# Input projections of a hybrid layer as seven block products per pair of column tiles (Strassen-Winograd), with block sums on GpSimd

## The chip, the cores and the metric

One Trainium2 chip, one core. The time is device microseconds of one execution of the program. The kernel before takes 1548.99 us, the median of 3 runs (1548.35 to 1551.43).

## The reference, cut to what matters

The layer takes 640 tokens (512 of one prompt, 8 x 16 of running streams), D = 1024, all float32. The change is in one product:

```
h = rmsnorm(x)                     # 640 x 1024
proj = h @ w_in                    # 1024 x 9064 columns
z, xbc, dt_raw, q, k, v, qi, ki, wi, g = split(proj)
xbc = silu(causal_conv(xbc, conv_state, conv_w, conv_b))     # 4 taps
y = rmsnorm(ssd_scan(...) * silu(z)) @ w_ssm_out             # branch a
o = dsa_attention(q, ...) @ w_attn_out                       # branch b
x = x + (sigmoid(g_a) * a + sigmoid(g_b) * b) @ w_o
x = x + hierarchical_moe(rmsnorm(x))                         # 32 experts
```

Of proj's columns, q (1024), x (2048), B and C (1024), z (2048) and the gates g (2048) make 64 column tiles of 128; each is produced as 128 output channels on the partitions by 640 tokens. k, v, ki, wi, dt and qi are projected otherwise and stay as they are.

## The kernel before, in words

The normalised, transposed input lies in SBUF as `hT` (128 x 8 x 640: 8 slices of the contraction, tokens along the free dimension). Weights pass through `wring`, a ring of three 2 MB slots (8 slices x 512 columns, four column tiles); `Ring` holds the order of the loads and the key whose products must be full before a slot is loaded anew, and SyncE (`chunks`) issues them in that order, between its other loads. `product` runs the 8 matmuls of one tile, `claim` waits until the PSUM bank of the tile before was read, `filled` signals it. `plan_banks` and `plan_group` deal out the 8 PSUM banks. A tile of q, x, B/C or z takes 8 matmuls of 512 columns (prompt) into one bank and 8 of 128 columns (streams) into a part of another; a tile of the gates takes 16 matmuls of 320 columns in two halves (`halves`).

Each engine works through one list of instructions, written by hand:

- TensorE (L1275 on): k/v, qi, transposes; query tiles 0 and 1 between the indexer's score products (`query`, L1317); indexer of the streams; query tiles 2 to 7; then four groups (`ssd_pe`, L989), each with x (4 tiles), B/C (2), z (4) and the SSM scan in 5 token tiles; gates of the first half; attention (`attention_pe`); then the dense part: branch outputs, with the gates of the second half; w_o with the router; the experts.
- ScalarE copies projections out of PSUM (`copy`, L1744; `ssd_act`, L1595): x, B and C into `raw` (two buffers of 667 columns, with the conv's old rows, L1626 and L1631), z into `zT`; after the convolution it applies Silu (L1638, L1639), and it forms the decays (`decays_act`, L1696), which come back over DRAM (`load_decays` on SyncE). `gate_act` (L1727) applies the sigmoid to gate tiles on the way out of PSUM.
- VectorE (`ssd_dve`, L1908) runs the convolution of each tile as 4 instructions (L1920, L1922) into one accumulator `acc`, and between them rounds of the top-k selection of the indexer (`top`, L2334: MAX8 and MATCH_REPLACE8, 80 rounds; `TOP_EARLY` and `TOP_UPTO` say how many run where).
- GpSimd gathers conv rows (L886), forms x * dt (L901), adds up squares (L942), issues output DMAs.

```
def product(out, chunk, m0, m, rhs, n, ks=KD, first=True, last=True):
    ...   # L1281: one matmul per slice k, all into one bank
for j in range(4):            # ssd_pe
    o = claim(pe, ("xbc", g, j))
    filled(product(o, w, j * P, P, prompt, TP), ("xbc", g, j))
```

Of the kernel before, what the change touches and what calls it, by code (L numbers as in the profile page):

```python
# [45 lines left out]
TOP_EARLY = (0, 24, 53)  # L46
TOP_UPTO = (53, 57, 65, 73, ROUNDS)
# [57 lines left out]
class Ring:  # L105
# [3 lines left out]
    def __init__(self, slots):  # L109
        self.slots, self.job, self.order, self.loads = slots, {}, [], [0] * slots  # L110

    def add(self, key, used, parts):
        s = len(self.order) % self.slots
        self.loads[s] += 16 * len(parts)
        self.job[key] = (s, self.loads[s])
        self.order.append((key, used, parts))


def plan_banks():
# [15 lines left out]
    b.add(("q", 0), any8)  # L135
    for i in range(1, 4):
        for h in range(IH):
            b.add(("pd", i, h), any8)
        if i == 2:
            b.add(("q", 1), any8)  # L140
# [15 lines left out]
    for c in range(2):  # L156
        for t in range(2 if c == 0 else 4, 4 * c + 4):
            b.add(("q", t), (2, 3, 4, 5, 6, 7))
        b.add(("qS", c), (2, 3, 4, 5, 6, 7))
# [13 lines left out]
    for s in range(-1, SB + 1):  # L173
# [6 lines left out]
        if s >= 1:  # L180
# [4 lines left out]
            b.add(("do", s - 1), (6, 7))  # L185
    for n in range(2):
        for what in ("b", "a") if n == 0 else ("ga", "gb", "a", "b"):
# [26 lines left out]

def plan_group(b, g):

    lo, hi = (0, 1, 2, 3), (4, 5, 6, 7)
    b.add(("cT", g), lo)
    b.add(("xbc", g, 0), lo)
    if g:  # L220
        b.add(("yt", g - 1), lo)
    b.add(("xbcS", g, 0), hi)
    for j in range(1, 4):
        b.add(("xbc", g, j), lo)
# [6 lines left out]
    b.add(("xbcS", g, 1), hi)  # L231
    for j in range(4, 6):
        b.add(("xbc", g, j), lo)
    for j in range(3):
        b.add(("z", g, j), lo)
    b.add(("cO", g, 0), hi)
    b.add(("cO", g, 1), hi)
    b.add(("bt", g, 0), hi)
    b.add(("bt", g, 1), hi)
    for step in range(NT + 1):  # L240
        if step < NT:
            b.add(("xt", g, step), lo)
            b.add(("cb", g, step), hi)
        if step == 0:
            b.add(("z", g, 3), lo)
        elif step == NT - 1:
            b.add(("zS", g), hi)
        if step > 0:
# [3 lines left out]
            if tt < SMP:  # L252
                b.add(("st", g, tt), hi)
            b.add(("yo", g, tt), lo if tt < SMP else (0,))
    for half in range(2):
        for j in range(2 * half, 2 * half + 2):
            for i in range(2):
                b.add(("s0", g, j, i), (1, 2, 3))
            if j == 0:
                b.add(("so", g), hi)  # L260
# [6 lines left out]
    if g == GROUPS - 1:  # L267
        b.add(("yt", g), lo)
        for c in range(4):
            for h in range(2):  # L270
                b.add(("ga", 0, c, h), lo)
        for c in range(4):
            for h in range(2):
                b.add(("gb", 0, c, h), lo)
# [4 lines left out]
def hybrid_layer(nc, x_prompt, x_sample, cache_k, cache_v, cache_kidx, state_conv, state_ssm,  # L279
# [9 lines left out]
    ring = Ring(3)  # L289
# [2337 lines left out]
```

## Time and profile before

| what | value |
|---|---|
| median of 3 runs | 1548.99 us |
| the profiled execution's own time | 1552.75 us |
| its span in the profile | 1551.0 us |
| granted TensorE clock, mean | 0.961 |
| TensorE busy | 1416.6 us, 91% |
| VectorE / ScalarE / GpSimd busy | 649.9 / 459.6 / 222.2 us |

The profile counts a float32 matmul of the program as two records, so 8 matmuls of a tile are "x16". Stages in us from the start of the span: 0 to 124 norm, k/v, indexer; 124 to 180 query tiles 2 to 7; 180 to 653 the four groups; 653 to 722 first gates; 722 to 882 attention; 882 to 1158 dense part; 1158 to 1257 w_o and router; 1257 to 1512 experts; then the output.

### The profile page before, as it was taken

Reading aid. Unit: us, or ns where it says so; the run is one execution under the profiler, and the core shown is the slowest. Engines: PE = TensorE matmul, PEld = TensorE weight load, DVE = VectorE, ACT = ScalarE, POOL = GpSimd, SP = SyncE. Lnnn points to the kernel's source line nnn. Section 1 sums busy time; section 2 is a strip of 40 time slices with the busy share of each in tenths; the row PEclk is TensorE's granted clock in tenths of the full one; section 3 lists DMA queues with packets and bytes.
Section 4 is the critical chain, followed back from the end, with each engine's and each line's share of the span. In section 5 each row is a group of like instructions: output and inputs, shape, how many; then the busy total and the mean of one; then the engine's idle time right before and its main releaser. Section 6 shows DMA issues by size and latency. Waiting matters only on the chain.

```text
span 1551.0 us, 19156 instructions
## 1 busy us (share of the span) xinstructions
PE 1416.6 (91%) x7458; PEld 895.4 (58%) x7458; DVE 649.9 (42%) x1435; ACT 459.6 (30%) x1059; POOL 222.2 (14%) x334
## 2 busy tenths in 40 slices
PE   7999999999999999999888899999999979878780
PEld 5545654764764764776566677777764545545440
DVE  3059962676776775802655511000013443211105
ACT  2161024652653653523655500010002211111112
POOL 3000000220220320312540000000000023222210
PEclk9999999999999999998999999999999979999885
DMA  8821313524433432707108420312036199999965
GB/s 235 221 80 32 109 55 99 163 94 127 148 108 102 152 111 68 198 15 232 23 17 185 152 99 0 109 55 55 0 119 264 45 363 414 415 416 415 414 262 210
DMA packets 135180, 247.43 MB, mean 160 GB/s; under 512 B 38836, under 2 KB 81572, under 8 KB 126164
## 3 DMA queue, kind: packets, MB, share of 16 engines
q1 hardware_dynamic: 124020, 215.10, 40.7%
q0 software_dynamic: 11072, 31.12, 5.6%
q8 instruction: 60, 0.98, 0.3%
q14 instruction: 28, 0.23, 0.0%
HBM read 216.50 MB, written 36.88 MB: 163 GB/s over the span
## 4 chain that ended last, share of the span: by engine, by line
PE 82%; DVE 5%; ACT 5%; issue 4%; DMA 3%; POOL 1%; SPq 0%; DVEq 0%; ACTq 0%; POOLq 0%
PE psum L1281 50%; PE psum L1559 9%; PE psum L1285 5%; PE psum L1459 4%; PE psum L1575 4%; PE psum L1313 2%; ACT arena L1744 2%; ACT arena L1823 1%; DVE arena L2053 1%; PE psum L1230 1%; PE psum L1185 1%; PE psum L1266 1%; PE psum L1090 1%; DVE arena L2468 1%; PE psum L1084 1%
## 5 line engine op out<-in xcount | busy, mean ns | idle before, releaser
L1281 PE MATMUL psum<-hT,wring 128*128 128x512 f32 (+2 forms) x2176 | 596.0, 436 | 0.7 <-issue 0.7
L1281 PEld LDWEIGHTS psum<-hT,wring 128*128 128x128 f32 x2176 | 349.7, 192 | 237.6 <-issue 196.9
L1285 PE MATMUL psum<-ident,arena 128*128 128x128 f32 (+3 forms) x950 | 141.2, 285 | 37.9 <-ACT arena L1744 12.5
L1285 PEld LDWEIGHTS psum<-ident,arena 128*128 128x128 f32 (+3 forms) x950 | 105.8, 143 | 96.2 <-issue 64.7
L1744 ACT ACTIVATE arena<-psum 128x512 f32<-128x512 f32 (+8 forms) x199 | 96.9, 535 | 198.4 <-PE psum L1281 138.0
L1281 PE MATMUL psum<-arena,wring 128*128 128x320 f32 x512 | 138.1, 431 | 0.0
L1281 PEld LDWEIGHTS psum<-arena,wring 128*128 128x128 f32 x512 | 96.6, 189 | 41.2
L1559 PE MATMUL psum<-wring,arena 128*64 128x256 f32 x608 | 79.2, 419 | 25.5 <-issue 21.7
L1559 PEld LDWEIGHTS psum<-wring,arena 128*64 128x64 f32 x608 | 52.2, 151 | 47.9 <-issue 27.8
L2475 DVE TENSOR_TENSOR arena<-psum,arena 128x128 f32<-128x128 f32 x32 | 9.3, 291 | 162.9 <-ACT arena L1893 157.4
L2398 DVE TENSOR_TENSOR arena<-psum,arena 128x320 f32<-128x320 f32 x16 | 7.9, 491 | 156.1 <-PE psum L1281 156.1
L1459 PE MATMUL psum<-wring,arena 128*128 128x512 f32 x160 | 70.6, 595 | 0.0
L1281 PE MATMUL psum<-oT,wring 128*128 128x320 f32 x256 | 69.3, 433 | 0.4 <-issue 0.4
L1922 DVE SCALAR_TENSOR_TENSOR arena<-arena,pc 128x664 f32<-128x664 f32 x72 | 67.5, 937 | 2.6
L2341 DVE MAX8 ssq<-arena 128x8 f32<-128x1040 f32 (+3 forms) x80 | 66.5, 832 | 1.9
L962 POOL DMA_DIRECT2D x_rows<-arena x5 | 2.7, 546 | 438.6 <-ACT arena L1886 438.6
L2342 DVE MATCH_REPLACE8 arena<-ssq,arena 128x1040 f32<-128x1040 f32 (+3 forms) x80 | 65.2, 815 | 0.0
L1893 ACT ACTIVATE arena<-psum 128x128 f32<-128x128 f32 x32 | 8.9, 277 | 179.5 <-PE psum L1559 166.4
L1575 PE MATMUL psum<-arena 128*64 128x512 f32 x256 | 61.0, 592 | 0.4 <-ACT arena L1895 0.4
L1281 PEld LDWEIGHTS psum<-oT,wring 128*128 128x128 f32 x256 | 48.6, 190 | 20.7 <-issue 0.6
L983 POOL DMA_INDIRECT y_rows<-arena,slot_row x32 | 32.4, 1011 | 186.6 <-ACT arena L1901 149.9
L2053 DVE CUSTOM_DVE_ANT_0 arena<-psum,arena 128x256 f32<-128x256 f32 (+3 forms) x64 | 43.3, 726 | 24.0 <-PE psum L1230 18.7
(321 smaller groups left out, 1543.7 us busy)
## 6 DMA issues: line engine op xcount, KB each, us to landing
wring<-in_w SPq DMA_DIRECT2D x38, 1024.0 KB
arena<-in_w SPq DMA_DIRECT2D x32, 1024.0 KB
wring<-in_w_in SPq DMA_DIRECT2D x13, 2048.0 KB, 7.7
hT<-in_w SPq DMA_DIRECT2D x14, 1024.0 KB
oT<-in_w SPq DMA_DIRECT2D x12, 1024.0 KB
arena<-a_rows SPq DMA_DIRECT2D x20, 512.0 KB, 4.3
arena<-in_state_ssm SPq DMA_DIRECT2D x16, 512.0 KB, 7.1
out<-arena POOLq DMA_DIRECT2D x16, 512.0 KB, 4.2
```

Of the source, the lines that this page charges most:

```text
L983: pool.indirect_dma_start(y_rows[:, :], bass.IndirectOffsetOnAxis(ap=slot_row[:, e:e + 1], axis=0), ysl[:, e % RS, :], None, bounds_check= ...
L1281: ins = mm(out, chunk[:, k, m0:m0 + m], rhs(k), start=first and k == 0, stop=last and k == ks - 1)
L1285: return nc.tensor.transpose(out, in_, ident[0:rows, 0:rows])
L1313: ins = mm(o[:, 0:SW], hT[:, k, tt * P:(tt + 1) * P], w[:, k, 0:SW], start=k == 0, stop=k == KD - 1)
L1459: ins = mm(o, mrg[:, k, t * P:(t + 1) * P], ws[n][:, k, :], start=k == 0, stop=k == KD - 1)
L1559: ins = mm(pbank(2 + e % 2)[h * SLOTS:(h + 1) * SLOTS, 0:FF].rearrange("p (c f) -> p c f", c=2), hgT[:, e % 2, k, :], w13[e % XS][:, :, k, ...
L1575: ins = mm(pbank(4 + e % 2)[m * SLOTS:(m + 1) * SLOTS, :], heT[:, e % 2, k, :], w2s[e % XS][:, k, HD2 * m:HD2 * (m + 1)], start=k == 0, st ...
L1744: release(fn(out, in_, ACT.Copy), key)
L1922: ins = stt(out=a, in0=r[:, w:w + 664], scalar=cw_col[:, w, ct:ct + 1], in1=a, op0=ALU.mult, op1=ALU.add)
L2053: release(nc.vector.tensor_tensor_reduce(out=out, in0=scores, in1=bias, scale=-ATT_SCALE, scalar=3.0e38, op0=ALU.add, op1=ALU.min, accum_o ...
L2341: link(nc.vector.max(top8, scores))
L2342: link(nc.vector.match_replace(scores, top8, scores, TAKEN))
```

## The change

Two neighbouring column tiles (256 columns) form a pair; there are 32 pairs: 4 of q, 5 in each of the four groups (x, x, B/C, z, z), 8 of the gates. A pair is split in blocks: the contraction in two halves of 4 slices, the tokens in two halves of 320, the columns in two tiles. Instead of 8 block products (32 matmuls of 320 columns) it takes seven, in the order 1, 5, 6, 3, 7, 2, 4, of 4 matmuls each. Products 1, 6, 7 and 4 go on adding into one bank, 5 and 3 into another, 2 has a third. After 1, 5 and 6 ScalarE copies the bank's present content to SBUF; VectorE forms three of the four output blocks as PSUM plus such a copy, and ScalarE copies the fourth:

```
SEVEN = (1, 5, 6, 3, 7, 2, 4)

def sum_weights(pool, key):
    ...
    tt_(s1, w[:, 0:4, P:2 * P], w[:, 4:8, P:2 * P], ALU.add).then_inc(S["sums_ready"], 1)
    tt_(s2, s1, w[:, 0:4, 0:P], ALU.subtract).then_inc(S["sums_ready"], 1)
    tt_(s4, w[:, 4:8, 0:P], s2, ALU.subtract).then_inc(S["sums_ready"], 1)
    tt_(w[:, 0:4, P:2 * P], w[:, 0:4, 0:P], w[:, 0:4, P:2 * P], ALU.subtract).then_inc(S["sums_ready"], 1)

def dense(pe, key, steps=SEVEN):
    w, (s1, s2, s4) = slot(key), weight_sums(key)
    terms = {1: (w[:, 0:4, 0:P], top_l), 5: (s1, row_sums[0]), 6: (s2, row_sums[1]), 3: (s4, low_r),
             7: (w[:, 0:4, P:2 * P], top_r), 2: (w[:, 4:8, 0:P], low_l), 4: (w[:, 4:8, P:2 * P], row_sums[2])}
    for n in steps:
        o = claim(pe, key + (n,))
        ...
        for k in range(4):
            ins = nc.tensor.matmul(o[:, 0:TH], wt[:, k, :], rows[:, k, :], start=n in (1, 5, 2) and k == 0,
                                   stop=k == 3, skip_group_check=True)
        filled(ins, key + (n,))

def pair_added(dve, key, n):          # n = 3, 7, 2
    held, i, h = {3: (6, 0, 1), 7: (5, 1, 1), 2: (1, 0, 0)}[n]
    for dst, a, b in homes(key, i, h):
        ins = nc.vector.tensor_tensor(dst, like(dst, bank(key + (n,))[:, a:b]), like(dst, stage(key, held)[:, a:b]), ALU.add)
    release(ins, key + (n,))

def pair_staged(act, key, n):         # n = 1, 5, 6: bank -> SBUF, 320 columns
def pair_crossed(act, key, fn_=ACT.Copy):     # n = 4
```

`claim` of a product that goes on in a bank waits until the product before it in that bank was read. `sum_rows` makes, once, three sums and one difference of blocks of `hT` (each 128 x 1280) on GpSimd, after the last use of qi; the block `top_r` of `hT` is overwritten.

The ring has four slots; the pairs use slots 0 and 1 in turn, each with 1 MB of weights, its sums and the staged copies beside them; a pair's weights are loaded when the pair before the last is done. Row sums lie in slot 2, slot 3 is `hT` after its last use.

Order: the pair q0 takes the places of query tiles 0 and 1 (4 products, then 3); in a group the first x pair is split by the turned stream rows and conv rows, the second z pair by scan steps 1 to 3. The gates of the second half move ahead of both branch outputs, which now run b, a, b, a (before: b, a, gates, a, b). `sum_weights` stands on GpSimd some 10 to 20 us of TensorE work ahead of its pair. Squares and gains of group g - 1 move behind the first x pair of group g, the decays of token tile 1 behind x pair 2. The top-k rounds are dealt out anew:

```
-TOP_EARLY = (0, 24, 53)
-TOP_UPTO = (53, 57, 65, 73, ROUNDS)
+TOP_Q = (22, 23, 24, 25, 26, 33, 39)
+TOP_GROUP = (46, 56, 59, 62, 65)
+TOP_GATES = (69, 74, 79, ROUNDS)
```

The experts' weight buffers are renumbered (first `wring` slot 1, then `oT`, slots 2 and 0, `hT`; before `hT` first).

TensorE, start of group 1's x tiles, before (L1281 is a projection, L1285 a transpose):

```order
L1281 MATMUL psum<-hT,wring 128x512 [waits free0,slot_loaded1]
L1281 MATMUL psum<-hT,wring 128x512 x7
L1285 MATMUL psum<-ident,arena 128x128 [waits free1,free0]
L1285 MATMUL psum<-ident,arena 128x128 x3
L1281 MATMUL psum<-hT,wring 128x128 [waits free5]
L1281 MATMUL psum<-hT,wring 128x128 x31
L1281 MATMUL psum<-hT,wring 128x512 [waits free2]
L1281 MATMUL psum<-hT,wring 128x512 x7
```

The same place now, products 5, 6, 3, then 7, 2, 4 of the first x pair (L639 is `dense`):

```order
L639 MATMUL psum<-wring 128x320 [waits sums_ready,free1]
L639 MATMUL psum<-wring 128x320 [waits sums_ready,free3]
L639 MATMUL psum<-hT,wring 128x320 [waits sums_ready,free1]
L1417 MATMUL psum<-ident,arena 128x128 [waits free0]
...
L639 MATMUL psum<-hT,wring 128x320 [waits sums_ready,free3]
L639 MATMUL psum<-hT,wring 128x320 [waits free2]
L639 MATMUL psum<-wring 128x320 [waits free3]
```

Each row now stands for a product of four matmuls; banks 3 and 1 come back after one other product, where before a bank came back after some tiles.

VectorE, group 1's x tiles, before (L1920/L1922 conv, L2341/L2342 a top-k round):

```order
L1993 TENSOR_TENSOR oT<-oT,psum 128x4x128 [waits free0,full1]
L1997 SCALAR_TENSOR_TENSOR oT<-arena,dcol,oT 128x640 [waits free1]
L1997 SCALAR_TENSOR_TENSOR oT<-arena,dcol,oT 128x640 [waits dve_chain] x3
L2000 TENSOR_TENSOR oT<-oT,arena 128x2560 [waits z_ready,dve_chain]
L1920 TENSOR_SCALAR arena<-arena,pc 128x664 [waits xs_ready,raw_ready]
L1922 SCALAR_TENSOR_TENSOR arena<-arena,pc 128x664 [waits dve_chain] x3
L2341 MAX ssq<-arena 128x8
L2342 MATCH_REPLACE arena<-ssq,arena 128x1040 [waits dve_chain]
L1920 TENSOR_SCALAR arena<-arena,pc 128x664 [waits xs_ready,raw_ready,dve_chain]
```

The same place now (L607 is `pair_added`; the convs are L2095/L2097, the rounds L2565/L2566), from the y rows of group 0 to the adds of the second x pair:

```order
L2201 SCALAR_TENSOR_TENSOR oT<-arena,dcol,oT 128x640 [waits dve_chain] x3
L607 TENSOR_TENSOR arena<-psum,wring 128x192 [waits gathered,full1,conv_done,free3,full0,dve_chain]
L607 TENSOR_TENSOR arena<-psum,wring 128x8x16
L607 TENSOR_TENSOR arena<-psum,wring 128x192 [waits full3,gathered,free1,conv_done,full0]
L2211 TENSOR_TENSOR oT<-oT,arena 128x2560 [waits z_ready]
L607 TENSOR_TENSOR arena<-psum,wring 128x320 [waits free3,full2]
L2095 TENSOR_SCALAR arena<-arena,pc 128x664 [waits free2,xs_ready,free1,raw_ready]
...
L2095 TENSOR_SCALAR arena<-arena,pc 128x664 [waits xs_ready,free3,raw_ready]
L2097 SCALAR_TENSOR_TENSOR arena<-arena,pc 128x664 [waits dve_chain] x3
L607 TENSOR_TENSOR arena<-psum,wring 128x192 [waits full1,free0,gathered,conv_done]
```

VectorE's reads of PSUM now stand between its convs and rounds, and two convs follow one another where a round stood between them.

## Rows read from the trace of the kernel before

**Rows 1.** The page: busy us, share of the span, instructions; and slices of 38.8 us, tenths.

```profile
PE 1416.6 (91%) x7458; PEld 895.4 (58%) x7458; DVE 649.9 (42%) x1435; ACT 459.6 (30%) x1059; POOL 222.2 (14%) x334
...
PEclk9999999999999999998999999999999979999885
```

**Rows 2.** The chain that ended last, in order: start us, us, what.

```profile
40.38 34.61 PE psum L1281 x128
...
243.45 5.55 DMA a_rows<-arena
...
317.34 65.66 PE psum L1281 x224
...
882.43 275.86 PE psum L1281 x1024
```

**Rows 3.** Stretches: us, busy (instructions) of PE, PEld, DVE, ACT, POOL; PEclk, DMA share, GB/s.

```profile
75.00:125.00 50.00, 47.22 (x231) 22.34 (x230) 29.85 (x80) 29.68 (x73) 0.00 (x0) 0.97 0.22 64
125.00:181.00 56.00, 56.00 (x231) 33.04 (x230) 52.50 (x129) 5.14 (x16) 0.32 (x3) 1.00 0.08 21
317.00:431.00 114.00, 112.71 (x617) 68.64 (x615) 78.67 (x122) 55.83 (x126) 21.94 (x36) 1.00 0.38 121
882.00:1158.00 276.00, 275.57 (x1026) 193.93 (x1025) 34.59 (x47) 10.58 (x20) 0.00 (x0) 1.00 0.22 73
265.00:275.00 10.00, 8.94 (x22) 4.61 (x23) 2.28 (x4) 9.89 (x26) 1.04 (x1) 0.66 1.05 260
```

**Rows 4.** Timeline of TensorE: start us, us, line, op, count [idle before, releaser].

```profile
265.35 1.20 PE L1285 MATMUL psum<-ident,arena 128*128 128x128 f32 x9 [2.00 <-ACT arena L1639]
...
267.26 0.80 PE L1061 MATMUL psum<-arena 128*128 128x128 f32 x2 [0.70 <-ACT arena L1744]
267.85 9.77 PE L1281 MATMUL psum<-hT,wring 128*128 128x512 f32 x16
```

**Rows 5.** Groups by form, ScalarE: busy us, mean ns, idle before.

```profile
L1744 ACT ACTIVATE arena<-psum 128x512 f32<-128x512 f32 x146 | 81.5, 597 | 196.8 <-PE psum L1281 138.0 <-PE psum L1285 57.2 <-PE psum L1342 1.6
L1733 ACT ACTIVATE arena<-psum 128x320 f32<-128x320 f32 x32 | 13.8, 437 | 108.4 <-PE psum L1281 101.5 <-DVE oT L2000 4.2 <-POOL arena L942 2.6
```

**Rows 6.** Groups by form, VectorE and GpSimd.

```profile
L2398 DVE TENSOR_TENSOR arena<-psum,arena 128x320 f32<-128x320 f32 x16 | 7.9, 491 | 156.1 <-PE psum L1281 156.1
L901 POOL TENSOR_TENSOR arena<-arena 128x512 f32<-128x512 f32 x20 | 20.8, 1041 | 146.7 <-DVE arena L1950 146.7
L942 POOL TENSOR_TENSOR arena<-arena 128x640 f32<-128x640 f32 x15 | 20.3, 1350 | 70.9 <-ACT arena L1687 70.0
```

**Rows 7.** Timeline of VectorE, group 1.

```profile
318.10 3.65 DVE L1997 SCALAR_TENSOR_TENSOR oT<-arena,dcol,oT 128x640 f32<-128x640 f32 x4
...
334.52 1.24 DVE L2341 MAX8 ssq<-arena 128x8 f32<-128x1040 f32 x1
...
337.13 0.57 DVE L1920 TENSOR_SCALAR arena<-arena,pc 128x664 f32<-128x664 f32 x1
337.73 2.80 DVE L1922 SCALAR_TENSOR_TENSOR arena<-arena,pc 128x664 f32<-128x664 f32 x3
...
385.60 2.11 DVE L1964 TENSOR_TENSOR arena<-arena 128x512 f32<-128x512 f32 x2
...
405.11 1.29 DVE L1964 TENSOR_TENSOR arena<-arena 128x512 f32<-128x512 f32 x2
```

**Rows 8.** Timeline of GpSimd, group 1.

```profile
385.52 1.04 POOL L901 TENSOR_TENSOR arena<-arena 128x512 f32<-128x512 f32 x1 [21.73 <-DVE arena L1950]
```

**Rows 9.** Timeline of ScalarE, group 1.

```profile
332.38 1.28 ACT L1638 ACT_TABLE_LOAD   x1
334.64 0.72 ACT L1638 ACTIVATE arena<-arena,pc 128x512 f32<-128x512 f32 x1 [0.98 <-DVE arena L1922]
...
388.07 2.44 ACT L1720 ACTIVATE arena<-arena 128x128 f32<-128x128 f32 x8
```

**Rows 10.** The page, DMA issues: line, engine, count, KB each, us to landing.

```profile
wring<-in_w_in SPq DMA_DIRECT2D x1, 1024.0 KB, 7.0
```

More of the change, by code:

```diff
@@ L155, in plan_banks @@
             b.add(("di", 1), (1,))
[L156 to L159, printed above, removed]
+    for i in range(1, 4):
+        plan_pair(b, ("q", i), (2 if i % 2 else 5, 3, 4))
     for g in range(GROUPS):
@@ L212, in plan_banks, with plan_pair @@
     return b
+def plan_pair(b, key, banks, steps=SEVEN):
+    acc, other, third = banks
+    for n in steps:
+        b.add(key + (n,), (acc if n in (1, 6, 7, 4) else other if n in (5, 3) else third,))
 def plan_group(b, g):
     lo, hi = (0, 1, 2, 3), (4, 5, 6, 7)
-    b.add(("cT", g), lo)
-    b.add(("xbc", g, 0), lo)
+    plan_pair(b, ("x", g, 0), (3, 1, 2), (1, 5, 6, 3))
     if g:
[L221 to L224, printed above, removed]
+        b.add(("yt", g - 1), (0,))
+    b.add(("cT", g), (7,))
+    plan_pair(b, ("x", g, 0), (3, 1, 2), (7, 2, 4))
+    plan_pair(b, ("x", g, 1), (0, 1, 2))
     if g == 0:
@@ L230, in plan_group @@
             b.add(("ar", i), hi)
[L231 to L239, printed above, removed]
+    plan_pair(b, ("bc", g), (3, 1, 2))
+    plan_pair(b, ("z", g, 0), (0, 1, 2))
+    b.add(("cO", g, 0), (7,))
+    b.add(("cO", g, 1), (4,))
+    b.add(("bt", g, 0), (5,))
+    b.add(("bt", g, 1), (6,))
     for step in range(NT + 1):
@@ L267, in plan_group @@
     if g == GROUPS - 1:
[L268 to L274, printed above, removed]
+        b.add(("yt", g), (0,))
+        for i, what in enumerate(("ga", "ga", "gb", "gb")):
+            plan_pair(b, (what, 0, i % 2), (0 if i % 2 else 3, 1, 2))
         for i in range(2):
@@ L727, in _ @@
                     load_decays(0, 1)
+                chunks(("z", g, 1))
+                after = [("x", g + 1, i) if g + 1 < GROUPS else ("ga", 0, i) for i in range(2)]
                 for tt in range(2, NT):
@@ L1315, in _ @@
             pe.wait_ge(consts, 3)
-            def query(t):
-                w = wait_chunk(pe, ("wq", t // 4))
-                o = claim(pe, ("q", t))
-                filled(product(o, w, (t % 4) * P, P, prompt, TP), ("q", t))
             w = wait_chunk(pe, ("wqi",))
@@ L1911, in ssd_dve, with conv @@
             y = yb[:, g % 2, :, :]
-            for j in range(6):
+            def conv(key, j):
                 u = 6 * g + j
@@ L2383, in _ @@
             newton(rt, rr, mrg[:, 0, :])
+            for what in ("ga", "gb"):
+                for i in range(2):
+                    for n_ in (3, 7, 2):
+                        pair_added(dve, (what, 1, i), n_)
             def merge(m, j):
```

610 lines of the change are left out of this document (393 added, 217 removed).

## The prediction

> **What bounds the kernel now.** I began with the page. TensorE is busy 91% of the span, the others 42, 30 and 14%, and its clock is granted at nine tenths or more in the slices of the four groups and the dense part [rows 1]. The chain of waits says the same by place: over a whole run of projections in a group it stays on TensorE for 65.66 us, and in the dense part for 275.86 us [rows 2]. The table of stretches shows that inside those stages TensorE idles hardly at all (112.71 of 114 us busy in group 1, 275.57 of 276 in the dense part) at a granted clock of 1.00, its upper level of 2.4 GHz [rows 3]. So a matmul less there is time less, and what can spoil it is an engine that hands a bank back late. VectorE is the one to watch: 52.50 of 56 us busy beside the query tiles, 78.67 of 114 in a group [rows 3].
>
> **What is removed.** The 34.61 us piece holds qi: 32 matmuls of 512 and 32 of 128 columns (two records each), so a couple costs 34.61 / 32 = 1.082 us [rows 2]. The dense part is 512 matmuls of 320 columns in 275.86 us, 0.539 each [rows 2]. A pair of q, x, B/C or z took 16 couples, 17.31 us; it takes 28 x 0.539 = 15.09, 2.22 less. A pair of the gates took 32 x 0.539 = 17.24, 2.15 less. 24 x 2.22 + 8 x 2.15 = **70.5 us** off TensorE.
>
> **What is added, and what hides it.** ScalarE makes four copies of 320 columns a pair, 4 x 0.437 = 1.75 us, where two tiles took 2 x 0.597 and two short ones: no more than before; the gates get sigmoids out of SBUF on top, hidden by 15 us of matmuls a pair [rows 5]. VectorE gets three adds a pair, at 0.491 for 320 columns; one that is split in two parts lies between that and twice that, and I take 0.65 [rows 6]: 1.8 us a pair, 58 us in all. GpSimd gets four sums of 512 columns a pair, 4 x 1.041 = 4.2 us, 133 us in all, and 4 x 2 x 1.35 = 10.8 us of row sums [rows 6]; it was busy 222 of 1551 us. The weights of a pair (1 MB) took 7.0 us to land in the one load of that size [rows 10]. 7.0 + 4.2 = 11.2 us is less than the 15.1 us of the pair between, and SyncE's `chunks` now waits for the pair before the last, so the sums should be in time; if that cover went, each pair would wait some us. The loads are the same bytes. The experts' buffers are renumbered, but as before two of five come free with w_o: nothing. The moves of squares, gains and gates cost nothing where TensorE has matmuls queued.
>
> **What the short banks cost.** Products are 4 x 0.539 = 2.16 us. A bank is wanted back one product after it was filled. ScalarE needs 0.44 for that; VectorE stands in longer work. Product 4 wants its bank 6 x 2.16 = 12.9 us after the pair's start, so VectorE must be at adds 3 and 7 (1.3 us) by 11.6. It comes from the last add of the pair before at about -1.7. Between stand two convs of 0.57 + 2.80 = 3.4 us, one Silu of 0.72 (with the streams' part about 1.1) before the second may use `acc` [rows 7, 9], and ScalarE first stages product 5, which ends at 4.3. The second conv so starts at 4.3 + 0.4 + 1.1 = 5.9, or 7.1 with a table load of 1.28 [rows 9], and ends at 9.3 to 10.5. In groups 1 to 3:
> - second x pair, no top-k round before it: in time.
> - B/C and first z pair, one round of 2.6 (334.52 to 337.13 [rows 7]): 11.9 to 13.1, late by 0.3 to 1.5; I take 0.9 each. ScalarE also has decays before B/C's conv (2.44 and more [rows 9]); bounds 0 and 3.
> - first x pair: the turned stream rows come at 9.7 us; behind them stand one operation of y of 512 columns and four of 640, 3.65 us [rows 7], then the adds 3 and 7: read at 14.9 instead of 14.0, late by 0.9.
> - second z pair, inside the scan: its staging holds up ScalarE's decays; nothing to 3 us, I take 1.5.
> - GpSimd beside VectorE: with a GpSimd sum running (385.52, 1.04 us [rows 8]) two SBUF-to-SBUF operations of VectorE took 2.11 us, without one 1.29 [rows 7]: 0.8 lost per sum. The conv is such an operation. If all four sums of three pairs lie beside convs it is 9.8 us a group; part of it falls where VectorE waits for Silu anyway. I take 2.4, bounds 0 and 9.8.
>
> That is 0.9 + 1.8 + 1.5 + 2.4 = 6.6 a group, **+19.8** for three. The Trainium skill (SBUF — State Buffer, "Who interferes with whom") makes it an exclusive lock: a VectorE instruction with two SBUF inputs waits out a GpSimd instruction that reads SBUF. By that rule the 0.8 would be up to 1.04, and the sum 2 us higher; the rows lie a little under it.
>
> Group 0: the second x pair has two rounds of the prompt before it (late 1.3, taken as half a round of the streams), B/C's three are covered by the small products of dt between; z's two rounds make it late by 3.5 (10.5 + 5.2 - 11.6 = 4.1 at most, 2.9 at least): 4.8. Its second z pair 1.5, contention 0.8. Given back is a wait of before: SyncE was held by a load's bank wait and wrote the decays only at 243.45 [rows 2]; TensorE then stood 2.00 and 0.70 us for ScalarE, and the next 8 matmuls took 9.77 us where 8 x 512 / 320 x 0.539 = 6.9 is full speed [rows 4], the clock granted there being 0.66 [rows 3]. In the new order that `chunks` waits only for an x pair. 2.0 + 0.7 + 2.9 = 5.6 back; net **+1.5**.
>
> Start: q0 stands in the indexer, where TensorE was busy 47.22 of 50 us and VectorE feeds the chain [rows 3]. Its row sums come one after the other, 2.7 us each, from the last use of qi; VectorE gets 1.8 us more: **+3** (0 to 6). Query pairs 1 to 3: rounds are cut into pieces so that the adds come in time, 7 fewer run before the groups: 0 (to 3). Gates: before the first ones 4 or 5 rounds, 13 us, just inside; after attention VectorE has the norm's reciprocal before the first adds; ScalarE a table load: **+3** in all (1 to 6).
>
> **Sum:** -70.5 + 19.8 + 1.5 + 3 + 3 = -43.2. Against the profiled execution's 1552.75 that is 1509.6; the median of the runs lies 3.8 below it, so **1506 us**. A change of 0.2% (3.1 us) is about what a measurement of this kernel can tell from none.
>
> **Rivals.**
> - *TensorE stays the bound, waits nearly vanish.* For it: the deadlines above are missed by about 1 us only. Against: they are missed on paper. -70.5 + 4 leaves 1482.
> - *VectorE becomes the bound in the groups.* All GpSimd sums beside convs and the upper bounds of the lateness: 3 x (0.9 + 3.0 + 3 + 9.8) = 50 and 5 more in group 0: 1505.8 - 19.8 + 50 + 5 = 1541. Against: VectorE's total in a group, 78.67 less five rounds (13) plus 9 of adds, stays well under 103. The Trainium skill (GPSIMD Engine Reference, "Engine selection") advises against this placing, saying two-input elementwise work belongs on VectorE, GpSimd being about 2x slower; by rows 1.041 against 0.65 (1.29 / 2) for 512 columns. On VectorE the sums would cost it 83 us more; that it isn't there speaks for the forecast.
> - *Short products don't run at 0.539.* If each of 224 products ends with a gap of 0.1 to 0.15 us because of its semaphores: 22 to 34 more, 1534. Against: the dense part changed bank every 8 matmuls at no visible cost.
> - *Slower: the clock.* Where waits grow to 2 us TensorE falls to its lower level, as at 265 to 275 [rows 3, 4]: 2.7 us of wait and 2.9 of clock. It decides if VectorE is late by 2 us or more at nearly every pair; at 20 pairs of the groups 20 x 5.6 = 112: 1552.75 - 3.8 - 70.5 + 112 = 1590. Against: group 1, with its 1.3 us of waits, keeps 1.00 [rows 3].
> - *The change does less than it says* (a pair falling back to eight products) is excluded: the listed rows show 28 matmuls a pair.
>
> **How the numbers follow.** Forecast 0.60, waits vanish 0.17, VectorE the bound 0.12, gaps 0.05, clock 0.06. The range of 1480 to 1534 takes in the first two, the gaps and half of the third. Faster: all but the clock and a little of VectorE's case, 0.93; same 0.02; slower 0.05.
>
> **What would show it.** The dense part about 267 us long (4 pairs and 384 matmuls: 60.4 + 206.9); groups 1 to 3 about 109.5 us each instead of 114 (114 - 5 x 2.22 + 6.6); TensorE's idle time in front of line 639 put down to VectorE's adds at line 607, 1 to 2 us at a time, at products 4; VectorE's convs longer than 0.94 us each where GpSimd's sums run; no clock below 0.9 in the groups. Waits of TensorE for `sums_ready` or weights would speak against my costing of GpSimd at nothing; a group at 103 us would make the second case right, one over 118 the third.

## The result, and the profile after

The changed kernel takes 1554.55 us (median of 20 runs, 1550.86 to 1560.32) against 1549.44 us before (20 runs, 1547.13 to 1552.84): ratio 1.0036, 95% interval 1.0027 to 1.0045. It is slower by 0.36%, where 1506 us had been forecast. The profiled execution took 1556.48 us, its span is 1554.9.

The page of the changed kernel, engines and granted clock (after the lines of [rows 1]):

```profile
PE 1368.6 (88%) x7202; PEld 911.9 (59%) x7202; DVE 741.7 (48%) x1563; ACT 480.1 (31%) x1095; POOL 420.6 (27%) x466
...
PEclk9999989999999999999799999999999979989995
```

TensorE is busy 48 us less than before and the span is no shorter: the time went from work into waiting. That it is 48 and not the 70.5 us of the removed products comes at least in part from products that ran at the lower clock, shown below. Columns of the next view: length of the stretch, busy time of each engine with its instructions, granted clock, DMA share, GB/s. The stretches are a part of group 0, group 1, group 2, and the dense part:

```profile
184.00:252.00 68.00, 50.66 (x183) 34.81 (x182) 47.15 (x85) 15.22 (x36) 18.44 (x22) 0.88 0.24 83
324.00:443.00 119.00, 106.13 (x571) 74.47 (x567) 83.98 (x128) 59.59 (x131) 53.82 (x57) 0.97 0.38 115
444.00:558.00 114.00, 104.18 (x567) 73.72 (x571) 82.49 (x128) 59.53 (x131) 53.70 (x57) 0.99 0.41 120
896.00:1163.00 267.00, 266.91 (x991) 187.52 (x992) 40.39 (x59) 14.12 (x27) 10.04 (x8) 1.00 0.29 91
```

Against [rows 3] the dense part is what was promised: 266.91 of 267 us busy, 8 us shorter. Group 2 is as long as group 1 before, but TensorE idles nearly 10 us of it; in group 0 it idles 17 of 68 us and the clock falls to 0.88. TensorE's waits by releaser (total, times, longest, us):

```profile
PE psum L639 <- DVE arena L607: 53.7, 20, 6.6
```

Line 639 is the block products, line 607 VectorE's adds. In the timeline all of the 53.7 us stand before product 4 of a pair. Three of them in group 0, from TensorE's timeline (start, length, in brackets the idle time before it and its releaser):

```profile
199.22 4.63 PE L639 MATMUL psum<-wring 128*128 128x320 f32 x8 [5.47 <-DVE arena L607]
...
221.52 3.98 PE L639 MATMUL psum<-wring 128*128 128x320 f32 x8 [4.03 <-DVE arena L607]
...
251.73 4.63 PE L639 MATMUL psum<-wring 128*128 128x320 f32 x8 [6.62 <-DVE arena L607]
```

Eight records of one product take 2.32 us at the upper level of the clock and 4.63 at the lower: after such a wait the product itself is paid up to twice.

From one first matmul of a stage to the next, in us (of the traces; a group runs to the next group's first x pair; before, group 0 is counted from its transposes, 0.5 us ahead of its first x product):

| stage | before | after | forecast of the difference | measured |
|---|---|---|---|---|
| up to the groups | 180.2 | 180.0 | -5.9 | -0.2 |
| group 0 | 129.5 | 144.3 | -9.6 | +14.8 |
| groups 1, 2, 3 | 114.1, 114.3, 113.9 | 119.6, 114.7, 114.7 | -4.5 each | +5.5, +0.4, +0.8 |
| first gates | 69.8 | 60.8 | -8.6 and part of +3 | -9.0 |
| attention | 160.6 | 161.9 | 0 | +1.3 |
| dense part | 275.7 | 267.5 | -8.6 and part of +3 | -8.2 |

So the gates give all that their products save, and the groups give back more than theirs: 44.6 us lie between forecast and measurement in the four groups, 24.4 of them in group 0 and 10.0 in group 1.

**How one pair of group 2 is late.** Its second x pair starts at 461.32, and product 4 should start 12.9 us later, at 474.3. VectorE's timeline of the changed kernel:

```profile
462.43 0.57 DVE L2095 TENSOR_SCALAR arena<-arena,pc 128x664 f32<-128x664 f32 x1 [0.30 <-ACT arena L1732]
463.04 2.80 DVE L2097 SCALAR_TENSOR_TENSOR arena<-arena,pc 128x664 f32<-128x664 f32 x3
469.27 0.91 DVE L2095 TENSOR_SCALAR arena<-arena,pc 128x664 f32<-128x664 f32 x1 [3.43 <-ACT arena L1751]
470.22 5.52 DVE L2097 SCALAR_TENSOR_TENSOR arena<-arena,pc 128x664 f32<-128x664 f32 x3
475.67 1.40 DVE L607 TENSOR_TENSOR arena<-psum,wring 128x192 f32<-128x192 f32 x5
```

The first convolution is done at 465.8. The second waits 3.43 us for Silu (line 1751), and then takes 6.4 us instead of 3.4. ScalarE in that time:

```profile
463.73 0.44 ACT L616 ACTIVATE wring<-psum 128x320 f32<-128x320 f32 x1 [0.75 <-PE psum L639]
464.07 2.42 ACT L1856 ACTIVATE arena<-oT 128x1280 f32<-128x1280 f32 x2
466.39 0.43 ACT L616 ACTIVATE wring<-psum 128x320 f32<-128x320 f32 x1
466.83 1.28 ACT L1750 ACT_TABLE_LOAD   x1
468.13 0.72 ACT L1750 ACTIVATE arena<-arena,pc 128x512 f32<-128x512 f32 x1
468.75 0.39 ACT L1751 ACTIVATE arena<-arena,pc 128x128 f32<-128x128 f32 x1
```

Behind the staging of product 1 stand the squares of the group before (line 1856, 2.42 us), the staging of product 5 and a table load; only then comes Silu. And GpSimd, all through the second convolution:

```profile
467.21 1.27 POOL L648 TENSOR_TENSOR wring<-wring 128x512 f32<-128x512 f32 x1 [3.20 <-DMA wring<-in_w_in]
468.55 1.27 POOL L650 TENSOR_TENSOR wring<-wring 128x512 f32<-128x512 f32 x1
469.90 1.42 POOL L652 TENSOR_TENSOR wring<-wring 128x512 f32<-128x512 f32 x1
471.28 1.88 POOL L653 TENSOR_TENSOR wring<-wring 128x512 f32<-128x512 f32 x1
473.12 6.73 POOL L1021 TENSOR_TENSOR arena<-arena 128x640 f32<-128x640 f32 x4
```

**The longest wait** is that before product 4 of group 0's B/C pair, which starts at 231.42 (product 4 due at 244.3, with adds 3 and 7 begun by 243.0). VectorE's timeline:

```profile
239.49 0.57 DVE L2095 TENSOR_SCALAR arena<-arena,pc 128x664 f32<-128x664 f32 x1 [4.69 <-ACT arena L1751]
240.10 2.80 DVE L2097 SCALAR_TENSOR_TENSOR arena<-arena,pc 128x664 f32<-128x664 f32 x3
242.81 1.24 DVE L2565 MAX8 ssq<-arena 128x8 f32<-128x1040 f32 x1
...
250.66 1.41 DVE L607 TENSOR_TENSOR arena<-psum,wring 128x192 f32<-128x192 f32 x5
```

Three rounds of 2.6 us stand between the second conv and the adds, and the adds begin 7.7 us late.

Three candidates follow: (A) the serial chain conv, ScalarE's queue, Silu, conv through the one accumulator; (B) GpSimd's sums and squares beside the convs; (C) too many rounds of the top-k selection before the adds.

### The profile page after: what moved, and what is told of

Read it like the earlier page. It is cut to its first block, busy times and chain, and to the rows that moved or that the text cites. A ratio compares the mean times of both kernels' runs of the same rounds, so it can differ in the third digit from the quotient of the medians.

```text
span 1554.9 us, 19411 instructions
## 1 busy us (share of the span) xinstructions
PE 1368.6 (88%) x7202; PEld 911.9 (59%) x7202; DVE 741.7 (48%) x1563; ACT 480.1 (31%) x1095; POOL 420.6 (27%) x466
## 4 chain that ended last, share of the span: by engine, by line
PE 68%; DVE 18%; ACT 6%; issue 4%; DMA 1%; POOL 0%; SPq 0%; DVEq 0%; ACTq 0%; POOLq 0%
PE psum L639 22%; PE psum L1413 16%; PE psum L1680 9%; PE psum L1417 5%; PE psum L1580 4%; PE psum L1696 4%; DVE arena L2097 3%; PE psum L1444 2%; DVE arena L2566 2%; ACT arena L1913 1%; DVE ssq L2565 1%; ACT arena L1990 1%; DVE oT L2201 1%; DVE arena L2166 1%; DVE arena L2272 1%
## 5 line engine op out<-in xcount | busy, mean ns | idle before, releaser
L639 PE MATMUL psum<-hT,wring 128*128 128x320 f32 x1024 | 292.5, 438 | 4.3 <-ACT arena L1939 3.9
L639 PE MATMUL psum<-wring 128*128 128x320 f32 x768 | 232.9, 455 | 53.8 <-DVE arena L607 53.7
L639 PEld LDWEIGHTS psum<-hT,wring 128*128 128x128 f32 x1024 | 195.6, 193 | 87.5 <-issue 6.3
L639 PEld LDWEIGHTS psum<-wring 128*128 128x128 f32 x768 | 150.2, 198 | 126.7 <-DVE arena L607 65.4
L1417 PEld LDWEIGHTS psum<-ident,arena 128*128 128x128 f32 (+3 forms) x950 | 106.9, 144 | 92.7 <-issue 63.6
L1913 ACT ACTIVATE arena<-psum 128x512 f32<-128x512 f32 (+8 forms) x155 | 72.0, 519 | 105.7 <-PE psum L1417 61.1
L1680 PE MATMUL psum<-wring,arena 128*64 128x256 f32 x608 | 84.3, 439 | 22.6 <-issue 20.8
L648 POOL TENSOR_TENSOR wring<-wring 128x512 f32<-128x512 f32 x32 | 43.7, 1367 | 217.6 <-DMA wring<-in_w_in 217.5
L2097 DVE SCALAR_TENSOR_TENSOR arena<-arena,pc 128x664 f32<-128x664 f32 x72 | 90.1, 1252 | 2.6
L2715 DVE TENSOR_TENSOR arena<-psum,arena 128x128 f32<-128x128 f32 x32 | 9.3, 291 | 160.6 <-ACT arena L2065 160.6
L2054 ACT ACTIVATE arena<-arena 128x1024 f32<-128x1024 f32 x5 | 5.3, 1057 | 232.3 <-DVE arena L2661 232.3
L616 ACT ACTIVATE wring<-psum 128x320 f32<-128x320 f32 x84 | 36.5, 434 | 111.4 <-PE psum L639 111.4
L2565 DVE MAX8 ssq<-arena 128x8 f32<-128x1040 f32 (+3 forms) x80 | 66.5, 831 | 1.9
L2566 DVE MATCH_REPLACE8 arena<-ssq,arena 128x1040 f32<-128x1040 f32 (+3 forms) x80 | 65.2, 815 | 0.0
```

The source lines that it names most:

```text
L616: release(nc.scalar.activation(stage(key, n), bank(key + (n,))[:, 0:TH], ACT.Copy), key + (n,))
L639: ins = nc.tensor.matmul(o[:, 0:TH], wt[:, k, :], rows[:, k, :], start=n in (1, 5, 2) and k == 0, stop=k == 3, skip_group_check=True)
L648: tt_(s1, w[:, 0:4, P:2 * P], w[:, 4:8, P:2 * P], ALU.add).then_inc(S["sums_ready"], 1)
L1417: return nc.tensor.transpose(out, in_, ident[0:rows, 0:rows])
L1680: ins = mm(pbank(2 + e % 2)[h * SLOTS:(h + 1) * SLOTS, 0:FF].rearrange("p (c f) -> p c f", c=2), hgT[:, e % 2, k, :], w13[e % XS][:, :, k, ...
L1913: release(fn(out, in_, ACT.Copy), key)
```

## The experiments

Each is the changed kernel with the edit shown, unless it says otherwise. "Groups" is the time from the first x pair of group 0 to the first gates in its trace (changed kernel 493.3; before 471.8). Two traces of one and the same kernel (below) differ there by 2 us, so less than some 3 us is not read. A trace is of one execution; in 9 that was 6 us above the median of its kernel, in 12 it was 8 below.

**1. No weight sums.**

```diff
-            tt_(s1, w[:, 0:4, P:2 * P], w[:, 4:8, P:2 * P], ALU.add).then_inc(S["sums_ready"], 1)
+            tt_(s1[:, :, 0:2], w[:, 0:4, P:P + 2], w[:, 4:8, P:P + 2], ALU.add).then_inc(S["sums_ready"], 1)
```

(and so for the other three; products 5, 6 and 3 take `w` in place of `s1`, `s2`, `s4`.)

> The weight sums on GpSimd are cut to 2 columns of each 128 (8 elements a partition instead of 512), and products 5, 6 and 3 read plain weights in their place; all semaphores, products, copies and adds stay. Left out: the weight sums. If GpSimd beside VectorE's convolutions is what makes product 4 late, the convs go back from 1252 to about 940 ns, each of groups 1 to 3 loses 6 us or more of its 114.6 to 119.6, and the time falls by 25 to 35 us, to about 1525. If VectorE is late because its second conv waits for ScalarE (staging of product 5, then Silu), the convs shorten all the same (some 7 us a group), but TensorE's waits at product 4 fall little and the time by under 12 us. If the rounds are it, group 0 keeps its waits of 4 to 6.6 us.

Measured: groups 460.8 us, 32.5 less; by group 133.2, 107.7, 109.7, 110.2. What is left out alters which experts the rows go to, so the total (2185.94 us) says nothing of the change; only the stages up to the dense part are read, here and in 5. The convs came only part of the way, to 1015 ns:

```profile
L2097 DVE SCALAR_TENSOR_TENSOR arena<-arena,pc 128x664 f32<-128x664 f32 x72 | 73.0, 1015 | 2.6
```

since GpSimd's squares (6.69 us for four) still lay beside the second conv. B is a cause. But the second x pair of groups 2 and 3 still made TensorE wait 2.07 us (1.25 in group 1), and group 0 kept waits of 5.47 and 6.62.

**2. No rounds in the groups.**

```diff
+                    if not TOP_GROUP[0] <= k < TOP_GROUP[-1]:
+                        link(nc.vector.max(top8, scores))
+                        link(nc.vector.match_replace(scores, top8, scores, TAKEN))
```

> The 19 top-k rounds that lie in the four groups are left out (46 to 64), those before and after stay. Left out: these rounds of the selection. If VectorE's rounds are what delays the adds, the four waits of 4 to 6.6 us in group 0 and the slow products behind them go (about 25 us), and 2 to 3 us in each of the others: about 1523. If the Silu chain alone or the contention alone sets product 4, group 0 still waits 2 us or more at each pair and less than 15 us come back.

Measured: 1525.52 us, ratio 0.9849 (0.9832 to 0.9865); groups 461.1, 32.1 less, 21 of it in group 0. C is a cause of the same size, and the estimate of 1523 held. The wait of 5.47 us before the first x pair's product 4 stayed: it belongs to rounds before the groups. The wait of 6.62 us of group 0's B/C pair is gone. The second x pair's wait stayed in groups 1 to 3 (2.53, 2.33, 2.35 us).

**3. Bank of the first query pair.**

```diff
-    plan_pair(b, ("q", 0), (5, 6, 7), (1, 5, 6, 3))
+    plan_pair(b, ("q", 0), (7, 6, 5), (1, 5, 6, 3))
```

(and so for steps 7, 2, 4.)

> The first query pair accumulates in bank 7 and has its third product in bank 5, so that product 1 does not wait for the bank that ScalarE still reads (the streams' indexer queries). If that wait (3.9 us) is a loss of its own, the first query pair's start comes 3 to 4 us earlier and so does all behind it: about 1550.5. If TensorE then only waits for the row sums of GpSimd (about 11 us of work from the last use of qi) or for VectorE's chain in the indexer, under 1 us comes back.

Measured: 1554.08 us, ratio 1.0031 (1.0019 to 1.0042) against the 1.0036 of the changed kernel. The wait of 3.9 us is gone, the first query pair starts 3.4 us earlier and the first x pair 2.0, and at the gates nothing of it is left (groups 495.3). The intervals of the two ratios allow a gain of up to some 4 us in all, so a small one is not excluded. Of the start stage this explains the wait, not the end time.

**4. Two accumulators.** The odd convs write into the scan's buffer `xw`, which is free then:

```diff
+        accs = [acc[:, 0, :], xw.rearrange("p u n -> p (u n)")[:, 0:664]]
-                if u:
-                    dve.wait_ge(S["xs_ready"], u)
-                a, r = acc[:, 0, :], raw[:, j % 2, :]
+                if u > 1:
+                    dve.wait_ge(S["xs_ready"], u - 1)
+                a, r = accs[j % 2], raw[:, j % 2, :]
```

(and Silu reads `accs[j % 2]` in place of `acc`.)

> The convolutions of odd tiles go to an accumulator of their own (the buffer of the scan, free there), so the second conv of a pair no longer waits for the first Silu, which stands on ScalarE behind the staging of product 5 of the next pair. All sums and rounds stay. If this chain is what makes VectorE late, the second conv starts up to 6 us earlier, the waits at product 4 in groups 1 to 3 vanish and those of group 0 shrink to the rounds' part: 20 to 35 us less, about 1525. If VectorE is late by the amount of its work (contention and rounds), it is idle less but its adds come hardly earlier: under 8 us.

Measured: 1513.40 us, ratio 0.9773 (0.9755 to 0.9790); groups 447.7, 45.5 less: 123.4, 106.9, 107.9, 109.5. VectorE in the second x pair of group 2 (it starts at 429.37):

```profile
430.49 0.57 DVE L2096 TENSOR_SCALAR arena<-arena,pc 128x664 f32<-128x664 f32 x1 [0.30 <-ACT arena L1733]
431.10 2.81 DVE L2098 SCALAR_TENSOR_TENSOR arena<-arena,pc 128x664 f32<-128x664 f32 x3
433.82 0.56 DVE L2096 TENSOR_SCALAR arena<-arena,pc 128x664 f32<-128x664 f32 x1
434.42 4.59 DVE L2098 SCALAR_TENSOR_TENSOR arena<-arena,pc 128x664 f32<-128x664 f32 x3
438.93 0.54 DVE L608 TENSOR_TENSOR arena<-psum,wring 128x192 f32<-128x192 f32 x2
440.50 0.56 DVE L608 TENSOR_TENSOR arena<-psum,wring 128x192 f32<-128x192 f32 x2 [1.04 <-PE psum L640]
```

The second conv starts 4.5 us after the pair instead of 8, and VectorE now waits for TensorE's products instead of the other way round. The mean conv is still 1241 ns long. The gain is more than the 20 to 35 us expected, and the largest that one edit gave: A is a cause.

**5. Two accumulators, no weight sums** (4 and 1 together).

> Two accumulators, and the weight sums cut to 2 of 128 columns (left out: the weight sums), products 5, 6 and 3 on plain weights. With one accumulator the sums' removal took 32 us off the four groups (493 to 461), the second accumulator 45 (to 448). If both only free the same slack before product 4, the two together give little over the larger: the groups take 442 to 446 us, the waits left are the first x pair's in group 0 (5.5) and B/C's there. If they are separate losses they add: 416 us or so, which is below what the matmuls take.  The waits of 1.94 us in the second z pair and 0.93 in the first x pair go in both cases, since they went with the sums before.

Measured: groups 433.3 (120.6, 104.4, 103.9, 104.4). One by one the two took off 45.5 and 32.5, together 60: neither separate losses (78) nor one and the same (45). My 442 to 446 was too high; 14.4 us of the sums' cost are left when the chain is gone. The waits of 1.94 us in the second z pairs vanished in both kernels without sums and in none other so far, so they come from GpSimd's sums in the scan.

**6. Two accumulators, no rounds in the groups** (4 and 2 together).

> Two accumulators, and the 19 top-k rounds of the groups left out (left out: these rounds). If rounds and Silu chain use up the same slack, the groups take 438 to 443 us against 448 with all rounds: only B/C's wait of 3.7 us in group 0 with the clock behind it and 2 to 3 us in groups 2 and 3 come back. If the rounds are a loss of their own, 20 us or more come back.

Measured: 1511.33 us, ratio 0.9755 (0.9737 to 0.9774), which overlaps that of 4; groups 447.8, nothing less; both of my cases, 438 to 443 and 20 us or more, missed. The B/C pair's wait in group 0 did go, but two products behind waits of 1.95 us took 4.09 and 3.85. The same 19 rounds that cost 32 us with one accumulator cost none that can be told with two.

**7. Two accumulators, the bank of 3, rounds dealt anew.** It is thirteen rounds (33 to 45), not seven, that stand before the first x pair's adds; nine stay there and four go behind the first two adds.

```diff
-TOP_GROUP = (46, 56, 59, 62, 65)
+TOP_GROUP = (46, 53, 57, 61, 65)
-            top(TOP_Q[5], TOP_GROUP[0])
+            top(TOP_Q[5], 42)
-                raws_added(("x", 0, 0), 0, (3, 7, 2))
+                raws_added(("x", 0, 0), 0, (3, 7))
+                top(42, TOP_GROUP[0])
+                raws_added(("x", 0, 0), 0, (2,))
```

> A whole kernel: two accumulators, the first query pair's banks turned as tried, and the top-k rounds dealt anew: of the 7 rounds before the first x pair's adds 4 go behind the first two adds, and group 0 has 7 rounds instead of 10, groups 1 to 3 have 4, 4, 4 instead of 3. If waits of 4 us and more are what costs in group 0 (the wait and the products behind it at the lower clock), 5 to 12 us more come off: about 1505. If VectorE's sum of work counts there, the waits only move to later pairs and the time stays at 1513 or a little under.

Measured: 1505.07 us, ratio 0.9708 (0.9689 to 0.9728). The first x pair's wait of 5.47 us is gone; 2.60 us of it came back at the next pair. The number is as expected, the place is not shown: the groups take 448.1 us against 447.7 in 4 (group 0 2.1 less, group 2 2.8 more), and the first x pair starts 3.6 us earlier.

**8. The kernel before with two accumulators** (`accs` and Silu's reads as in 4).

```diff
-                if u:
-                    dve.wait_ge(S["xs_ready"], u)
-                a, r = acc[:, 0, :], raw[:, u % 2, :]
+                if u > 1:
+                    dve.wait_ge(S["xs_ready"], u - 1)
+                a, r = accs[j % 2], raw[:, u % 2, :]
```

> The kernel before with the same second accumulator, nothing else changed. There TensorE waits for no conv in groups 1 to 3 (a tile's bank is read by ScalarE alone), so the chain from conv to Silu should cost nothing: 1549 within 0.2%. If the second accumulator is worth something by itself (shorter scan start, shorter group 0), it comes to 5 us or more less here too, and the gain of 41 us in the changed kernel is not all the change's own chain.

Measured: 1547.18 us, ratio 0.9982 (0.9971 to 0.9993): 2.7 us, at the edge of what can be told. The other 38 us of experiment 4 exist only in the changed kernel; that they exist because it ties TensorE's banks to VectorE's queue is what the waits at line 639 say.

**9. Only the new deal of rounds** (the edit of 7), one accumulator. The expectation also speaks of the bank of 3, but its edit is not in this kernel: its first query pair still waits 3.92 us for line 1939.

> The changed kernel with its one accumulator; only the first query pair's banks and the deal of the rounds are altered, as in the run with both. If lateness at product 4 is one budget that rounds, sums and the Silu chain spend together, part of what leaving out 19 rounds gave (29 us in all) comes by moving 3 of them and splitting 7: 8 to 15 us off, about 1543. If the chain alone rules in group 0, it stays above 1550.

Measured: 1540.68 us, ratio 0.9925 (0.9897 to 0.9952); groups 481.9. As expected of a shared budget: 14 us for three rounds moved and thirteen split, nine and four.

**10. Number 7, with GpSimd's work moved.**

```diff
+                    if j % 2:
+                        pool.wait_ge(S["conv_done"], u + 1)
                     if j == 1:
                         sum_weights(pool, ("bc", g))
-                        if g:
-                            squares(g - 1)
                     elif j == 3:
                         sum_weights(pool, ("z", g, 0))
+                        if g:
+                            squares(g - 1)
-                    if tt == 3:
+                    if tt == 4:
                         sum_weights(pool, after[0])
```

> The version with two accumulators and the new deal of rounds; GpSimd now waits until the second conv of a pair is done before it forms the next pair's weight sums, forms the squares a pair later, and the sum in the scan one tile later, so that its sums run beside rounds and adds instead of convs. Without any sums the groups had 14.4 us less than with them. If the loss is contention by position, the convs return to about 0.95 us, the wait of 1.94 us in the second z pair goes, and 5 to 10 us come off (about 1498). If the sums then come too late, TensorE waits for them at product 5 and the time stays or grows.

Measured: **1490.54 us, ratio 0.9618 (0.9588 to 0.9649)**; groups 429.4 (110.2, 106.9, 106.4, 106.0), more than the 5 to 10 us that I had given it. VectorE in the second x pair of group 2, then GpSimd:

```profile
413.29 0.58 DVE L2098 TENSOR_SCALAR arena<-arena,pc 128x664 f32<-128x664 f32 x1 [0.30 <-ACT arena L1735]
413.90 2.80 DVE L2100 SCALAR_TENSOR_TENSOR arena<-arena,pc 128x664 f32<-128x664 f32 x3
416.62 0.56 DVE L2098 TENSOR_SCALAR arena<-arena,pc 128x664 f32<-128x664 f32 x1
417.21 2.80 DVE L2100 SCALAR_TENSOR_TENSOR arena<-arena,pc 128x664 f32<-128x664 f32 x3
421.15 0.56 DVE L608 TENSOR_TENSOR arena<-psum,wring 128x192 f32<-128x192 f32 x2 [1.13 <-PE psum L640]
```

```profile
420.10 1.27 POOL L649 TENSOR_TENSOR wring<-wring 128x512 f32<-128x512 f32 x1 [5.23 <-DVE arena L2100]
421.45 1.27 POOL L651 TENSOR_TENSOR wring<-wring 128x512 f32<-128x512 f32 x1
422.80 1.27 POOL L653 TENSOR_TENSOR wring<-wring 128x512 f32<-128x512 f32 x1
424.03 1.27 POOL L654 TENSOR_TENSOR wring<-wring 128x512 f32<-128x512 f32 x1
```

Conv and sums are apart and both run at their own speed; the mean conv is back where it was, and TensorE's waits for the adds are nearly gone:

```profile
L2100 DVE SCALAR_TENSOR_TENSOR arena<-arena,pc 128x664 f32<-128x664 f32 x72 | 67.4, 936 | 2.6
```

```profile
PE psum L640 <- DVE arena L608: 4.2, 5, 1.2
```

**11. Number 7 once more,** for the comparison in the same series.

> The version with two accumulators and the new deal of rounds once more, unchanged, for the comparison on the same chip: 1505, within 3 us. Against it the kernel with moved sums is read.

Measured: 1506.10 us, ratio 0.9707 (0.9677 to 0.9736), groups 446.1 against 448.1 in its first trace. So the moved sums and squares of 10 are worth 15.6 us.

**12. Only GpSimd's work moved** (edit of 10), one accumulator, the change's own rounds.

> The changed kernel with its one accumulator and its own deal of rounds; only GpSimd's work is moved: sums after the second conv, squares a pair later, the scan's sum one tile later. If sums and squares beside the convs are a cause of their own, the convs return to 0.95 us here too, group 2 and 3 fall from 114.7 to 108 to 110 us, and 20 to 30 us come off (about 1528). If the second conv, which here ends 12 us after the pair's start or later, pushes the sums behind TensorE's need, product 5 waits for them and less than 10 us come off.

Measured: 1531.17 us, ratio 0.9886 (0.9869 to 0.9902); groups 462.4 (136.0, 108.8, 109.0, 108.6). Position alone is worth 23 us, as much within the groups (30.9, in the fastest of its five runs) as leaving the sums out (32.5). The expected time and groups 2 and 3 held, and TensorE did not wait at product 5; the convs did not come back to 0.95 us but to 1049 ns on average.

This run also settles the second x pair. In group 2 it starts at 441.29:

```profile
449.25 0.57 DVE L2097 TENSOR_SCALAR arena<-arena,pc 128x664 f32<-128x664 f32 x1 [3.43 <-ACT arena L1753]
449.85 2.80 DVE L2099 SCALAR_TENSOR_TENSOR arena<-arena,pc 128x664 f32<-128x664 f32 x3
452.57 0.55 DVE L607 TENSOR_TENSOR arena<-psum,wring 128x192 f32<-128x192 f32 x2
```

The second conv waits the same 3.43 us for Silu and starts 7.96 us after the pair, as in the changed kernel; it takes 3.4 us, the adds begin at 11.3, and TensorE does not wait, in none of groups 1 to 3. The chain as it stands is just in time when GpSimd keeps away from the conv.

## Why the prediction was wrong

**The saving was right.** Products run at 4 x 0.539 = 2.155 us with no gap between them (that rival falls), the dense part takes 267.5 us against 267 forecast, the gates give 17.2 us in all, and nothing is seen of the 3 us that I had added there. ScalarE's staging and the weights came in time, as costed. The place of the trouble was named too: line 639 waits for line 607 at products 4. What failed is the size of these waits: 52.2 us of them in the groups, and the slow products behind them, where the forecast had 19.8 + 7.1 = 26.9 us of lateness.

**The first step that failed is the second x pair ("in time").** Its second conv was to start at 5.9 or 7.1 us and end by 10.5; it started at 7.95 and ended at 14.4. ScalarE's two squares (2.42 us), which this change puts between the stagings of products 1 and 5, were not in my chain ("the moves of squares ... cost nothing"), and the conv took 6.4 us beside GpSimd instead of 3.4. TensorE waits 2.3 to 2.7 us there in groups 1 to 3. With a second accumulator (experiment 4) these waits vanish, sums and rounds untouched; but they vanish too in experiment 12, where only GpSimd's work is moved and the conv starts as late as before: 7.95 + 3.4 = 11.35 is inside the 11.6. So the late start and the longer conv make this pair late only together, and the larger error is the conv's 3 us. How much of the late start the squares make was not measured by a run.

**The contention was sized at a quarter of its bound.** I took 2.4 us a group between bounds of 0 and 9.8. The changed kernel's conv steps by form:

```profile
L2097 DVE SCALAR_TENSOR_TENSOR arena<-arena,pc 128x664 f32<-128x664 f32 x72 | 90.1, 1252 | 2.6
...
L2095 DVE TENSOR_SCALAR arena<-arena,pc 128x664 f32<-128x664 f32 x24 | 18.9, 787 | 59.7 <-ACT arena L1751 47.2 <-ACT arena L1732 11.5 <-DVE arena L607 0.8
```

Against 0.93 (2.80 for three) and 0.57 of [rows 7], the 18 and 6 steps of a group cost 18 x 0.32 + 6 x 0.22 = 7.1 us more; and 47.2 us of idle time end with line 1751, Silu; in the kernel before it was 31.2, so at most a part of it is new. I had argued that part of it falls where VectorE waits for Silu. In the pair above 2 of some 6 us of sums do: GpSimd's sums start when the weights land (467.21) and run on through the second conv, which begins at 469.27, behind the Silu. The squares, moved by the change to the same place, were not counted. And a weight sum alone takes 1.27 us, not 1.04: GpSimd is busy 198 us more than before, where I had 144. The first z pair is late by 3.3 to 3.7 us instead of 0.9. Experiments 1, 5, 10 and 12 show this term.

**Group 0, the largest miss (24.4 us): deadlines were not worked out.** "7 fewer run before the groups: 0" looked at the total. Thirteen rounds of 1.52 us run back to back between the last add of the query and the first of x, from 178.44 to 198.15, and product 4 was due at 192.9. That is the wait of 5.47 us; four more of 1.9 to 6.6 follow. The longest is that of the B/C pair, whose three rounds I took as "covered by the small products of dt": they stand behind its second conv, 6.62 us are waited, and without rounds (experiment 2) the wait is gone. I had 4.8 + 1.5 + 0.8 us for the group; the waits at product 4 are 23.5, and the four slow products behind them add 8.6 (4.63, 3.98, 4.63 and 4.63 for 2.32). The 5.6 us given back at the decays did come: behind the first z pair, from 279.20 on, TensorE's timeline has neither the wait of 2.00 nor that of 0.70, and the next product takes 2.32 us. 23.5 + 8.6 - 5.6 is 26.5; the group took 25.9 more than its products alone would have it.

**Groups 1 to 3.** The waits are 11.5, 8.9 and 8.5 us against 6.6. The first x pair was right: 0.9 forecast, 0.92 to 0.93 measured. The second z pair took 1.94 to 1.95 for 1.5. B/C's pair waited only in group 1 (2.61).

**The terms were added, but they share one budget.** Each lateness counts only beyond the slack before product 4, and then in full. So a cause measured alone gets what the others have pushed over the edge: second accumulator 45.5, no sums 32.5, no rounds 32.1 us of the groups, 110 in sum, where experiment 10, which has the accumulator, the sums moved and the rounds dealt anew (429.4), gives 64. And once the chain is gone, 19 rounds cost nothing (experiment 6). On paper, my terms stood near the edge, so errors all on the late side could not cancel.

**The rivals.** VectorE did become what sets the groups, but not by its total (82.49 of 114 us busy in group 2): by its order and its waits. The clock rival was right in mechanism and limited to group 0 and single pairs. The rival in which the waits nearly vanish (1482 us) is what experiment 10 comes near to, 1490.5. Of the signs that I had named, the clock below 0.9 came (0.88, in part of group 0), and of the groups after group 0 one passed 118 us.

**Start.** Forecast -5.9 up to the first x pair, measured -0.2. 3.9 us of it is a wait I had not seen: the first query pair's product 1 wants the bank that ScalarE still copies the streams' queries from. With that wait taken away (3, 7, 10 and 11) the first x pair starts at 176.1 to 178.0, in the other traces at 179.0 to 181.5: some 3 us. Why no gain is seen in the total of experiment 3, and where the other 2 to 3 us of the forecast went, stays open.

## What to carry to other kernels

When a change makes TensorE's banks come free through another engine's queue, write down for each deadline the whole queue of that engine and of the one that it waits for in turn, with everything that the change moved there; near the edge, take the upper bounds. Look first for a buffer that makes two engines alternate: doubling one accumulator of 664 columns was worth 41 us here. And work given to GpSimd costs by its position: the same sums and squares beside two-input VectorE work or a few us later are 16 to 23 us apart.

## What the runs showed of the hardware

- Contention stretches both engines and is neither free nor a strict turn-taking. Three conv steps take 2.80 us alone and 5.52 beside GpSimd; a sum takes 1.27 alone and up to 1.89. The Trainium skill (SBUF — State Buffer, "Who interferes with whom") calls the shared port an exclusive lock for a VectorE instruction with two SBUF inputs. The trace agrees in kind. In degree it is milder: from 470.22 to 475.74 VectorE did 2.80 us of lone work, and GpSimd the rest of the third sum (some 1.0 of 1.27), the fourth (1.27) and 2.6 of the 6.73 us of squares, which alone are 4 x 1.35: 2.1 if they ran evenly, 1.3 if only this part was slowed. That is an estimated 6.4 to 7.2 us of lone work in 5.52.
- The first step of a conv, a TENSOR_SCALAR with one SBUF tile and a scalar per partition, takes 0.57 us alone, 0.80 to 1.20 beside GpSimd's sums and 1.40 beside its squares.
- A GpSimd sum of 512 columns read as 4 x 128 takes 1.27 us; the row of the same size in the kernel before is 1.04 [rows 6]. I had costed all sums at the latter.
- After a wait of 4 us or more TensorE ran at its lower level for most or all of the next product in every case in group 0 (3.98 to 4.63 us for 2.32). After waits of about 2 us it sometimes did: 4.09 us after 1.95 in experiment 6, but 2.42 after 1.94 in the changed kernel, and 2.42 even after 3.66 in experiment 4.
